# Input projection by seven products per pair of weight tiles, with its operands prepared in the stage before

## The reference, cut to what matters

```python
D_MODEL, SEQ, HEAD_DIM, MEM_LEN = 1024, 2048, 64, 256   # BATCH = DEPTH = 1
# one layer; widths: A_Q 512, A_KV 128 (K and V), B 512 (Q, K, V): D_IN = 2304
h = rmsnorm(x, g_mix[l])
proj = h @ w_in[l] + b_in[l]                      # 2048 x 1024 x 2304
qa = rotary(proj[..., :s1], positions); ka = rotary(proj[..., s1:s2], positions)
va, qb, kb, vb = the remaining columns of proj
oa = window_sink_gqa(qa, ka, va, sinks[l])
ob = chunk_relbias_attention(qb, kb, vb, rel_bias[l])
x = x + concat([rmsnorm(oa), rmsnorm(ob)]) @ w_out[l]
x = x + memory_cross_attention(rmsnorm(x, g_cross), rmsnorm(mem, g_mem), w_cq, w_ckv, w_co)
x = x + (silu(h @ w_gate) * (h @ w_up)) @ w_down  # h = rmsnorm(x, g_ffn)
return rmsnorm(x, g_final)
```

## Time and profile before

| | us |
|---|---|
| median of three runs | 2965.98 (2959.81 to 2967.26) |
| the profiled execution's own time | 2965.04 |
| its span in the profile | 2963.2 |
| from the start to the projection's first matmul | 134.4 |
| from there to the projection's last matmul | 451.8 |
| from there to attention's first matmul | 19.6 |
| rest of the span | 2357.4 |

### The profile page before, as it was taken

How to read it: one execution, slowest core, us unless ns; L and a number is a source line. 1 busy time by engine, 2 the same in 40 slices (tenths; PEclk the granted TensorE clock), 3 DMA queues, 4 the chain that set the end, 5 groups by cost and what they waited for, 6 DMA issues and landing times. The chain is left out here.

```text
span 2963.2 us, 39417 instructions
## 1 busy us (share of the span) xinstructions
PE 2784.1 (94%) x14112; PEld 2353.4 (79%) x14112; DVE 1598.7 (54%) x2913; ACT 1063.8 (36%) x2101; POOL 1052.1 (36%) x756
## 2 busy tenths in 40 slices
PE   7898989979999899799998799999999998999998
PEld 7786868769999788688887588888788887788876
DVE  3247446457779533233333566666766665654354
ACT  5333333246666422233332333333333332222242
POOL 6644344311100011311222555555555553453152
PEclk9899999979999999899999899999999999999999
DMA  7655666476575433312223433335433333744454
GB/s 237 221 186 197 225 217 215 151 178 158 142 165 136 150 128 128 127 61 75 86 75 114 163 105 97 97 105 170 143 107 96 104 107 113 274 141 145 147 169 131
DMA packets 244535, 428.47 MB, mean 145 GB/s; under 512 B 17792, under 2 KB 151424, under 8 KB 239104
## 3 DMA queue, kind: packets, MB, share of 16 engines
q1 hardware_dynamic: 222416, 406.15, 43.0%
q10 hardware_dynamic: 21936, 19.93, 2.4%
HBM read 285.50 MB, written 135.27 MB: 142 GB/s over the span
## 5 line engine op out<-in xcount | busy, mean ns | idle before, releaser
L50 PE MATMUL gu_acc<-gu_t,shared_m 128*128 128x512 f32 x880 | 344.4, 391 | 10.0 <-DVE gu_t L2348 6.5
L51 PE MATMUL gu_acc<-gu_t,shared_m 128*128 128x512 f32 x880 | 343.9, 391 | 0.0
L52 PE MATMUL gu_acc<-gu_t,shared_m 128*128 128x512 f32 x880 | 343.7, 391 | 0.0
L334 POOL TENSOR_TENSOR front_wq_lo<-front_wq_raw,front_wq_hi 128x1024 fp32r<-128x1024 f32 x72 | 179.1, 2489 | 234.0 <-ACT front_wq_hi L330 233.4
L1424 PE MATMUL att_sum_o<-att_v,att_turned_sb 128*128 128x64 f32 x1616 | 203.0, 270 | 0.0
L50 PEld LDWEIGHTS gu_acc<-gu_t,shared_m 128*128 128x128 f32 x880 | 166.1, 189 | 46.2 <-issue 6.9
L1424 PEld LDWEIGHTS att_sum_o<-att_v,att_turned_sb 128*128 128x128 f32 x1616 | 197.2, 193 | 0.2
L52 PEld LDWEIGHTS gu_acc<-gu_t,shared_m 128*128 128x128 f32 x880 | 166.2, 189 | 34.6
L51 PEld LDWEIGHTS gu_acc<-gu_t,shared_m 128*128 128x128 f32 x880 | 166.1, 189 | 34.6
L1394 PE MATMUL att_sum_s<-att_k,att_q 128*128 128x320 f32 (+3 forms) x704 | 146.1, 327 | 25.4 <-DMA att_k<-qk_d 25.1
L330 ACT ACTIVATE front_wq_hi<-front_wq_raw 128x1024 fp32r<-128x1024 f32 x72 | 76.3, 1059 | 251.1 <-PE qkv_acc L52 149.1
(11 more groups left out here) (310 smaller groups left out, 7310.8 us busy)
## 6 DMA issues: line engine op xcount, KB each, us to landing
front_wq_raw<-in_w_in SPq DMA_DIRECT2D x72, 512.0 KB, 5.2
down_a<-a_d SPq DMA_DIRECT2D x37, 704.0 KB, 4.1
ahead_w_even<-in_w_gate SPq DMA_DIRECT2D x44, 512.0 KB, 4.4
more_w_odd<-in_w_up SPq DMA_DIRECT2D x44, 512.0 KB, 4.3
a_d<-gu_a_mix SPq DMA_DIRECT2D x88, 256.0 KB, 3.1
att_k<-qk_d SPq DMA_DIRECT2D x36, 512.0 KB, 13.2
a_d<-gu_a SPq DMA_DIRECT2D x66, 256.0 KB, 4.2
shared_m<-a_d SPq DMA_DIRECT2D x19, 704.0 KB, 4.3
```

The lines of the kernel that those rows point to most:

```text
L50: pe.matmul(out, l_hi, r_hi, start=first, stop=False)
L51: pe.matmul(out, l_hi, r_lo, start=False, stop=False)
L52: return pe.matmul(out, l_lo, r_hi, start=False, stop=last)
L334: pool.tensor_tensor(self.lo[:, i % Q_SLOTS, :], self.raw[:, i % Q_SLOTS, :], raw(self.hi[:, i % Q_SLOTS, :]), ALU.subtract).then_inc(self ...
```

## The change

The projection is formed with seven products instead of eight. `PAIRS_IN` lists 9 pairs of weight tiles (v values, u unrotated, r rotated, x keys to be rotated beside values), each formed for two halves of 1024 tokens: 18 pairs by 7 products by 4 inner blocks by 3 matmuls. The seven sums of token tiles, whatever the half, are now made in `stage_products`, for all 16 tiles, and stored to the new DRAM tensor th_d; `stage_qkv` loads them again, split, seven operands of 1 MB per half. The first two and the first weight pair are loaded and split within `stage_products` (class `FirstOperands`, which takes the place of `InWeights` and of `GateUpOperands`, whose content it keeps). Rotated heads are laid out so that the two halves of a head lie in the same partitions of two tiles, so the swap DMAs vanish; POOL makes the sine products. The tables are made once, over 128 partitions, in `stage_products`, and stored to trig_d. In `stage_products` m_d is now stored in 4 KB rows instead of 1 KB pieces, and `stage_mix` reads it with four DMAs in 1 KB pieces instead of two with 16 KB rows. `stage_attention` reads the rotated tiles with another stride. The bias table is made per head in 8 rounds instead of 4 heads at a time in 2.

```diff
+        def stage_at(j, steps):
+            return at_share((8 + 5.6 * j + steps) / 106)
+
+        TURN = [stage_at(j, 0) for j in range(NT)]
+        SCALE = [stage_at(j, -3) for j in range(NT)]
...
+        MIX = [stage_at(2 * i + 1, 5) for i in range(HT)]
+        PUT = [stage_at(j, 6) for j in range(NT)]
+        PUT_MIX = [stage_at(2 * i + 1, 12) for i in range(HT)]
+        TABLE = [at_share((20 + 4 * part) / 106) for part in range(6)]
+        AHEAD = at_share(0.75)
...
+                def mix_pair(i):
+
+                    dve.wait_ge(rows.s_lo, 2 * MT + 4 * i + 4)
+                    if i >= 2:
+                        dve.wait_ge(s_mst[i % 2], 48 * (i // 2))
...
+                    dve.tensor_tensor(t3, h22, h12, ALU.subtract).then_inc(s_mixed, 1)
+                    dve.wait_ge(s_mixed, 4 * i + 1)
+                    dve.tensor_tensor(h12, h12, h11, ALU.subtract).then_inc(s_mixed, 1)
+                    dve.wait_ge(s_mixed, 4 * i + 2)
+                    dve.tensor_tensor(t2, h22, h12, ALU.subtract).then_inc(s_mixed, 1)
+                    dve.wait_ge(s_mixed, 4 * i + 3)
+                    dve.tensor_tensor(t4, t2, h21, ALU.subtract).then_inc(s_mixed, 1)
...
+                def put(q, i, tile, semaphore):
+                    half, u = divmod(i, UNITS)
+                    sp.dma_start(t_d[q, half, :, u * BANK:(u + 1) * BANK], tile.rearrange("p k c -> p (k c)")
+                                 ).then_inc(semaphore, 16)
...
+                def sin_products(kp, z):
...
+                    for i, g in enumerate(reversed(ROTATE[z])):
+                        pool.tensor_tensor(turned_part[:, i, :], y[:, g, :], trig[:, 1, z, :], ALU.mult
+                                           ).then_inc(s_part, 1)
...
+                def rotate(kp, z):
...
+                    dve.wait_ge(s_part, 2 * r + 2)
+                    for g in (a, b):
+                        dve.tensor_tensor(y[:, g, :], y[:, g, :], trig[:, 0, z, :], ALU.mult).then_inc(s_cos, 1)
...
+                    if q == 5:
+                        result(2, bank, u3[:, :], ALU.add)
+                        dve.tensor_tensor(u2[:, :], bank, u2[:, :], ALU.add).then_inc(s_sum, 1)
...
-                    for k in range(KT):
+                    if kp % PAIRS == 0:
+                        pe.wait_ge(s_tlo, 2 * (kp // PAIRS * N_PROD + q) + 2)
+                    hi, lo = (part[q].rearrange("p (u k c) -> p k u c", k=KH, c=P) for part in (t_hi, t_lo))
+                    for k in range(KH):
                         wk = slice(k * P, (k + 1) * P)
-                        last = split3(pe, acc[i % ACCS][:, :], weights.hi[:, i % Q_SLOTS, wk],
-                                      weights.lo[:, i % Q_SLOTS, wk], hs[b % 2][0][:, k, :], hs[b % 2][1][:, k, :],
-                                      k == 0, k == KT - 1)
+                        last = split3(pe, acc[s % ACCS][:, :].rearrange("p (u c) -> p u c", c=P), w_hi[s % RS][:, wk],
+                                      w_lo[s % RS][:, wk], hi[:, k], lo[:, k], k == 0, k == KH - 1)
...
-                for part in range(2):
-                    k = slice(part * KT // 2, (part + 1) * KT // 2)
-                    act.dma_start(raw(m_sb[1][:, k, :].rearrange("p k c -> p (k c)")),
-                                  m_d[:, k.start * D:k.stop * D]).then_inc(s_m, 16)
+                for h in range(XH):
+                    act.dma_start(raw(m_sb[1][:, :, h * MEM:(h + 1) * MEM]),
+                                  m_d[:, h].rearrange("p b (k m) -> p (b k) m", k=KT // 2)).then_inc(s_m, 16)
```

More of the change, by code:

```diff
@@ L291, in high, with whole @@
                            ACT.Copy).then_inc(self.s_hi, 1)
+    def whole(self, act, n, out):
+        for b in range(2):
+            act.wait_ge(self.s_turned, 2 * n + b + 1)
+            act.activation(out[:, 4 * b:4 * b + 4, :], self.turned[b][:, :].rearrange("p (k t) -> p k t", k=4),
+                           ACT.Copy).then_inc(self.s_lo, 1)
     def low(self, dve, n, lo, hi):
@@ L301 @@
 BT = BANK // P
[L302 to L335, removed]
@@ L462, in _ @@
[L462 to L472 removed]
+                sp.dma_start(fr[:, :], freq).then_inc(s_fr, 16)
@@ L514, in _, with low @@
                     rows.rsqrt(pool, n)
-                for n in range(ITEMS):
+                def low(n):
                     pool.wait_ge(s_whi, n + 1)
@@ L543, in _ @@
                 for a in range(TOTAL):
+                    for j in range(NT):
+                        if a == SQUARE[j]:
+                            rows.square(act, MT + j)
+                        if a == WHOLE[j]:
+                            whole(j)
                     sums = acc[a % ACCS][:, 0:width(a)]
@@ new lines, in consumed, with result_at, summed, rot_index @@
+        def consumed(engine, s):
+            kp, q = split_at(s)
+            if q == 0:
+                engine.wait_ge(s_p1, kp + 1)
+            else:
+                engine.wait_ge(s_sum, READ[N_PROD - 1] * kp + READ[q])
+        def result_at(s):
+            kp, q = split_at(s)
+            return (kp, RESULT[q]) if 0 <= s < TOTAL and q in RESULT else (None, None)
+        def summed(engine, kp, g):
+            engine.wait_ge(s_sum, READ[N_PROD - 1] * kp + (1, 4, 5, 7)[g])
+        def rot_index(kp, z):
+            return 2 * sum(rotated(i) for i in range(kp)) + z
@@ new lines, in split_due @@
+        def split_due(s):
+            kp, q = split_at(s)
+            due = []
+            before, g = result_at(s - 1)
+            if before is not None and kind(before) == "u":
+                due.append((before, g))
+            if q == 0 and rotated(kp - 1):
+                due += [(kp - 1, g) for g in ROTATE[0]]
+            if q == 3 and rotated(kp - 1):
+                due += [(kp - 1, g) for g in ROTATE[1]]
+            return due
+        END = TOTAL + N_PROD
+        order = [what for s in range(END) for what in split_due(s)]
@@ new lines, in stage_qkv, with values_due, heads_of @@
+        place = {what: o for o, what in enumerate(order)}
+        value_order = [result_at(s) for s in range(TOTAL) if result_at(s)[0] is not None and values(split_at(s)[0])]
+        value_place = {what: v for v, what in enumerate(value_order)}
+        def values_due(s):
+            return [value_place[what] for lag, name in ((1, "x"), (2, "v")) for what in (result_at(s - lag),)
+                    if what in value_place and kind(what[0]) == name]
+        def heads_of(kp):
+            name = PAIRS_IN[kp % PAIRS]
+            return 1 if name == "x" else 2
```

1037 lines of the change are left out of this document (595 added, 442 removed).

## The result

The changed kernel takes 2977.1 us, median of 7 runs (2975.8 to 2979.5); the kernel before, on the same chip, 2966.8 (2959.8 to 2970.4). The ratio is 1.0032, 95% interval 1.0022 to 1.0042: slower by 0.3%, where 2915 was forecast.

The account below looks back on a forecast made before the run. PE, busy for 94% of the span, was taken as the bound. First stage +29.6, projection -76.8, handover -4 and `stage_mix` +1 gave -50.2 from 2965.0, so 2915 us, range 2886 to 2962.

Parts of the forecast that it names:

- First stage, +29.6 forecast: First stage: added work on DVE and DMA delays the projection's start to 164 us, +29.6 us.
- Sum 146.0: First stage: DVE's total work of 146.0 us, 140.8 of it after 16 us, so not done before 157.
- Sum 153.9: First stage: DMA's full work, old transfers plus added stores and loads, 153.9 us.
- The forecast's own signs: First stage: DVE over 85% busy, DMA share near 0.95, projection start near 164; wrong if before 152 or after 180.
- Rival B: First stage: POOL blocks DVE throughout, 46 us more, projection starts at 210, total 2961; chance 0.10.
- Projection, -76.8 forecast: Projection: fewer matmuls and transposes shorten it from 451.8 to 375 us, -76.8, with ends 360 and 390.
- D: Projection: matmuls reading four runs of 128 columns take 0.26 instead of 0.227 us, 50 us gone, total 2965; chance 0.03.
- C: Projection: DVE becomes the bound through 176 operations with both inputs in SBUF, at 1.78 us each total 2983; chance 0.05.
- the clock: Projection: allowance of 3.8 us for a slower clock on top of 353.5 us of PE work.
- the gaps: Projection: PE loses 12.7 us at the start and change of halves, plus 5 us of DVE stalls.
- PE waits in the middle of it: Projection: sign that the forecast is wrong, PE waiting mid-projection for sums that DVE owes; no size given.
- Handover and stage_mix: After the projection: shorter handover to attention, -4 us; slower loads of m_d in 1 KB pieces in `stage_mix`, +1 us.

Follow-up runs that it names:

- the best kernel: Changed kernel plus third x slot, x loads and h stores before weight loads, earlier mixed stores, squares, scalings, later value transposes, second-pair weights after operands 3 to 7: 2942.9 us.

## Why the prediction was wrong

**First stage, +29.6 forecast, +71.1 measured.** The step that failed is the end of the stage: it was taken from two sums of work, "Sum 146.0" for DVE and "Sum 153.9" for DMA, with 2.7 us "for waits of DVE". The waits passed on through ACT and SP were put at nothing, and they were PE's 53.9 us at the transposes of x. The forecast's own signs say so: DVE was busy for 56% where over 85 was named, the DMA share was 0.77 where 0.95 was, and the start lies beyond 180.
- DVE's sum was too high: 110.7 us. The scalings took 1.69 us on average where I took 2.89 (four rows of before, three of them slow, were too few), the chained subtractions 1.25 where I took 1.72. The groups, 16 to 205.5 us:

```profile
L273 DVE SCALAR_TENSOR_TENSOR prod_xn<-prod_x,prod_rs,prod_gain 128x1024 f32<-128x1024 f32 x16 | 27.1, 1693 | 17.7 <-POOL prod_rs L267 17.7
L645 DVE TENSOR_TENSOR prod_h<-prod_h 128x512 f32<-128x512 f32 x8 | 16.1, 2010 | 0.3
...
L643 DVE TENSOR_TENSOR prod_mixed<-prod_h 128x512 f32<-128x512 f32 x8 | 8.7, 1083 | 0.0
```

- DMA's sum was right: 158 us of work and 55.85 MB, for 153.9 and 55.6. But it was spread over 205.5.
- I had named SP's queue and then priced the wrong direction ("a late sum also delays weights"). What happened is that the weights' wait delays x and h. It was to be seen before: the earlier trace rows gave the bytes and POOL's pace, but SP's own waits in the kernel before, 16 to 134 us, which I had not read, have this at their head:

```profile
SPq L436 <- POOL prod_w_lo L517: 68.9, 26, 7.6
```

  That wait was nearly as long, with 4 tiles of x behind it and not 16 tiles and 64 more stores.
- Rival B came near to the start, 210 for 205.5, by a mechanism that did not occur: POOL slowing every sum. That was luck.
- What the edits show of the 41.5 us by which the start missed 164: the order of issue is worth 14.7, and with the slot, the places and the earlier squares and scalings it comes to 25.7 (179.8). Where the other 15.8 go stays open; no run gave the weights, whose wait still stands first (39.7 us of SP in the best kernel), more than four slots.

**Projection, -76.8 forecast, -56.4 measured.** The matmuls held: 0.227 us apart in the middle, so D fell. C fell too: DVE was busy for 293 us of the 331 forecast; its 512-column operations with both inputs in SBUF took 1.07 us on average where I took 1.2. The two terms that were mis-sized are the clock, 15.3 us (368.8 of PE less 353.5; by the distances between starts, some 11 of them lie in the first and third window of the projection above) in place of 3.8, and the gaps, 26.6 in place of 12.7 + 5. The better model stood in the earlier trace rows, in the projection of the kernel before: there PE was busy for 426.0 us with 411.1 of work, 14.9 more, and idle for 25.8. Both losses stayed, 40.7 us then and 41.9 now, where I had 21.5, so the projection saved just its matmuls and transposes, 57.6 us, less 1.2. `stage_gate_up` loses less at its ends: its clock is 0.92 and 0.93 in the earlier trace rows at the start and the change of halves, here it is 0.78 and 0.87, and PE is idle for 10.1 and 9.3 us in place of 6.2 and 6.5. The forecast named "PE waits in the middle of it" as a sign of error: there were few (241 to 400: 4.0 us idle).

**Handover and stage_mix.** -4 forecast, -4.5 measured. The +1 of `stage_mix` can't be told from the 2 us of the whole rest, which varies by more; ACT's wait for m_d is 2.5 us, as in the earlier trace rows.

**Range and chances.** Even the best kernel starts at 179.8, 16 us after the 164 of the forecast. The result lies above the range because no case held both losses: B had a start at 210 with the forecast's own projection of 375, C a long projection with the forecast's start. Start and projection missed by 41.5 and 20.4 us, together all of the 62 between 2915 and 2977.

## What to carry to other kernels

Two sums of work say when a stage can't be over; they don't say when it is. When a change puts more transfers into a queue that one engine issues in order, read that queue's own waits in the kernel before, and ask of each new transfer which wait it is written behind: moving x loads and h stores ahead of the weight load in the same place, with no instruction added, was worth 14.7 us here, more than a third buffer (5.8). And where one wait goes and another takes its place, as ACT's for x and for h did, look for what both stand behind. When the same kernel already runs the stage that changes, take its waits and its clock from there before you take them from a stage that only looks alike.

## What the runs showed of the hardware

- **The clock after a stop.** In the changed kernel the second to the thirteenth matmul of the projection are 0.427 us apart, at a granted clock of 0.50 (205.5 to 209.5 us), the 1.2 GHz level, after PE had stood for 4.81 us at the barrier. From the fourteenth on they are 0.23 apart. First, eleventh to thirteenth and fifteenth:

```profile
205.49 0.77 PE L50 MATMUL qkv_acc<-front_t,front_w 128*128 128x512 f32 x1 [4.81 <-PEq L87]
...
209.90 0.63 PE L51 MATMUL qkv_acc<-front_t,front_w 128*128 128x512 f32 x1
210.32 0.63 PE L52 MATMUL qkv_acc<-front_t,front_w 128*128 128x512 f32 x1
210.75 0.47 PE L50 MATMUL qkv_acc<-front_t,front_w 128*128 128x512 f32 x1
...
211.29 0.40 PE L52 MATMUL qkv_acc<-front_t,front_w 128*128 128x512 f32 x1
```

  A stop of PE so costs itself and here another 2.4 us (12 times 0.2) after it. The kernel before pays this too: 134.4 to 138.4 us is at 0.50 as well, after 4.5 us at the barrier.
- **The rate of one core.** Windows of this case reach 416 GB/s (216 to 222 us) and 395 over 40 us. The prediction set 358 GB/s from the Trainium skill against the trace; the Trainium skill ("Perfetto Trace Analysis", section "Roofline") says the share of 358 holds when both cores of a pair use the memory, and that one core alone can pull more, up to its DMA engines. With one core in use, the trace agrees with this.
- **DVE beside POOL.** The same chained subtraction took 2.01 us on average on one line and 0.95 to 1.08 on the three others, with POOL busy for 53% of the time: of the 32, 23 took 0.68 to 0.69 us and nine 2.28 to 2.87. The Trainium skill ("SBUF — State Buffer", section "Who interferes with whom") lets both exclude each other for a whole instruction; in this trace it costs time in nine of 32, not every time.
